# Four modulation blocks asked for at once, and x behind them, at the start of a flow-matching layer kernel

## The reference, cut to what matters

```python
def layer(x, cond, k_ctx, v_ctx, w_ada, b_ada, w_in, ...):
    mods = (jax.nn.silu(cond) @ w_ada + b_ada)[:, None, :]
    sh1, sc1, ga1, sh2, sc2, ga2 = jnp.split(mods, 6, axis=-1)
    u = x * (1 + sc1) + sh1
    xc, bg, cg, q, k, v, g_conv, g_na = jnp.split(u @ w_in, IN_SPLITS, axis=-1)
    ...  # gated convolution, attention, merge by gates, w_o, layer norm
    x = layer_norm(ALPHA * x + ga1 * (merged @ w_o), ln1_g, ln1_b)
    u2 = x * (1 + sc2) + sh2
    x = layer_norm(ALPHA * x + ga2 * peer(u2, w_query, sub_keys, expert_u, expert_v), ln2_g, ln2_b)
```

## Time and profile before

| | us |
|---|---|
| median of 3 runs | 1949.89 |
| lowest and highest run | 1946.81, 1951.14 |
| span of the profiled execution | 1975.1 |
| TensorE busy in it | 1811.1 (92%) |
| VectorE busy in it | 1291.4 (65%) |
| GpSimd busy in it | 908.3 (46%) |
| ScalarE busy in it | 283.3 (14%) |
| moved by DMA in it | 670.23 MB, 339 GB/s on average |

### The profile page before, as it was taken

One profiled execution on the slowest core, in us unless ns is written; L12 is line 12 of the kernel. 1 busy time (PEld: TensorE's weight loads), 2 busy tenths in 40 slices (PEclk: granted clock), 3 DMA queues, 4 the chain that ended last, 5 costly groups with the idle time before them and its releaser, 6 DMA issues.

```text
span 1975.1 us, 21712 instructions
## 1 busy us (share of the span) xinstructions
PE 1811.1 (92%) x8148; PEld 1170.2 (59%) x8148; DVE 1291.4 (65%) x2583; ACT 283.3 (14%) x660; POOL 908.3 (46%) x837
## 2 busy tenths in 40 slices
PE   4888899967999899999999999998799899995997
PEld 2676744446544349997888888886544334442443
DVE  2110487879688778999988966549956533349752
ACT  0120010037300001111110100016620000000000
POOL 1010226668555412235454566657856664545500
PEclk8998999989999999999999999999999999997999
DMA  8894949898999967469999999997999999999983
GB/s 355 355 365 189 356 178 407 290 369 274 337 398 336 346 241 286 140 217 376 346 374 379 370 409 409 409 372 267 336 354 409 410 407 409 409 409 410 409 326 135
DMA packets 166713, 670.23 MB, mean 339 GB/s; under 512 B 19370, under 2 KB 19498, under 8 KB 160972
## 3 DMA queue, kind: packets, MB, share of 16 engines
q0 software_dynamic: 112512, 410.79, 55.1%
q1 hardware_dynamic: 49344, 242.24, 31.3%
q10 hardware_dynamic: 4752, 15.81, 2.1%
HBM read 659.27 MB, written 7.39 MB: 338 GB/s over the span
## 4 chain that ended last, share of the span: by engine, by line
PE 65%; DMA 13%; DVE 8%; POOL 7%; issue 4%; another core or an unknown queue 2%; ACT 1%; ACTq 0%; SPq 0%; DVEq 0%; POOLq 0%
PE psum L853 22%; PE psum L921 16%; PE psum L1014 7%; DMA arena<-in_expert_u_dram,arena 7%; POOL arena L542 7%; PE psum L979 4%; PE psum L944 3%; PE psum L947 3%; DVE arena L1425 3%; PE psum L881 2%; DMA arena<-in_w_ada_dram 2%; PE psum L956 1%; PE psum L954 1%; PE psum L698 1%
## 5 line engine op out<-in xcount | busy, mean ns | idle before, releaser
L542 POOL DMA_INDIRECT arena<-in_expert_u_dram,arena x384 | 487.2, 1269 | 349.7 <-DVE arena L1425 219.5
L1425 DVE CUSTOM_DVE_ANT_0 arena<-arena 128x1024 f32<-128x1024 f32 x384 | 460.5, 1221 | 182.4 <-DMA arena<-in_expert_u_dram,arena 172.1
L542 POOL DMA_INDIRECT arena<-in_expert_v_dram,arena x384 | 382.3, 996 | 375.5 <-DVE psum L1659 208.6
L921 PE MATMUL psum<-arena 128*128 128x512 f32 x1024 | 451.4, 602 | 24.9 <-issue 16.9
L853 PE MATMUL psum<-arena 128*128 128x256 f32 x2048 | 445.9, 381 | 4.9 <-DMA arena<-in_expert_uT_dram 4.9
L1659 DVE SCALAR_TENSOR_TENSOR psum<-arena,psum 128x1024 f32<-128x1024 f32 x254 | 327.0, 1287 | 162.1 <-DMA arena<-in_expert_v_dram,arena 132.0
L853 PEld LDWEIGHTS psum<-arena 128*128 128x128 f32 x2048 | 390.7, 191 | 58.8 <-issue 5.2
L921 PEld LDWEIGHTS psum<-arena 128*128 128x128 f32 x1024 | 196.2, 193 | 281.1 <-issue 272.0
L1014 PE MATMUL psum<-arena 128*128 128x128 f32 x1280 | 149.8, 278 | 3.6 <-issue 3.1
L1014 PEld LDWEIGHTS psum<-arena 128*128 128x128 f32 x1280 | 147.3, 195 | 5.4 <-issue 4.7
L710 PE MATMUL psum<-arena 128*128 128x512 f32 x320 | 137.7, 592 | 0.0
(11 more groups left out here) (174 smaller groups left out, 1352.1 us busy)
## 6 DMA issues: line engine op xcount, KB each, us to landing
arena<-in_expert_uT_dram SPq DMA_DIRECT2D x128, 512.0 KB
arena<-in_expert_v_dram SPq DMA_DIRECT2D x128, 512.0 KB
arena<-in_w_in_dram SPq DMA_DIRECT2D x16, 2048.0 KB
arena<-in_w_ada_dram SPq DMA_DIRECT2D x12, 2048.0 KB
arena<-in_w_query_dram SPq DMA_DIRECT2D x8, 2048.0 KB, 22.9
arena<-in_w_in_dram SPq DMA_DIRECT2D x16, 512.0 KB, 8.7
arena<-in_w_o_dram SPq DMA_DIRECT2D x4, 2048.0 KB
arena<-in_expert_u_dram,arena POOLq DMA_INDIRECT x384
```

Source lines behind the costliest of these rows:

```text
L542: pool.indirect_dma_start(slot, None, table[0], bass.IndirectOffsetOnAxis(ap=number, axis=0)).then_inc(land, 16)
L921: mm = pe.matmul(bank(2 + 2 * d + hf), own, RINGS[value_load_of(n) % RING][:, hf * HALF:(hf + 1) * HALF], start=n == 0, stop=n == NKEYS - 1)
L1425: dve.tensor_tensor_reduce(UR[b], UR[b], U2B[e], 1.0, 0.0, ALU.mult, ALU.add, DOTS[e % 2][:, k:k + 1]).then_inc(u_free, 1)
```

## The change

The fourth modulation block gets the place at offset 31744, and is left out of the turns of the three slots. SyncE no longer waits for the small inputs. GpSimd waits for the small inputs as before, and then for the fourth modulation block, before it asks for x.

```diff
+SPARE = ("ada", 3)
...
         slot_of, before, last, counts, landed = {}, {}, {}, [0] * (WSLOTS + 1), {}
-        for n, key in enumerate(loads):
-            slot = n % WSLOTS
+        turns = [key for key in loads if key != SPARE]
+        for key in loads:
+            n = WSLOTS if key == SPARE else turns.index(key)
+            slot = WSLOTS if key == SPARE else (n + (n >= turns.index(("in", 1, PROJ[0])))) % WSLOTS
             if key[0:2] == ("query", 1):
                 slot = (2, 3, 0, 1)[key[2]]
...
         @block.sync
         def _(sp):
-            sp.wait_ge(cond_in, 48)
             for key in loads:
...
-                if slot_of[key] == 3:
+                if slot_of[key] == WSLOTS and key != SPARE:
                     sp.wait_ge(merge_done, 16)
...
             pool.dma_start(MODS, b_ada[0:1, :].partition_broadcast(2)).then_inc(bada_in, 16)
             pool.wait_ge(cond_in, 48)
+            pool.wait_ge(w_land[WSLOTS], 16)
             for k in range(KD):
                 pool.dma_start(UT[:, k, :], xT[k * P:(k + 1) * P, :]).then_inc(x_in, 16)
```

## The result

The changed kernel takes 1958.62 us in the median of 7 runs, the kernel before 1949.89 in 7 runs: a ratio of 1.0039, with a 95% interval of 1.0027 to 1.0051, so slower by 7.6 us (5.3 to 9.9); the two medians lie 8.7 us apart. Ratios compare fast executions alone, so one of e7 (3199 us, at a clock of 0.556) and one of the kernel before (1985 us) are not in them. I had forecast 1953.8 with a range of 1948.0 to 1958.5: the right side, half the size. By the ratio the changed kernel stands at 1957.5, inside the range; its median is 0.1 us above the range's end.

The account below looks back on a forecast made before the run. An unbroken chain of waits starts with full DMA engines, the first projection needing modulation and x. Extra bytes ahead of x, 8.8 us, less 4.9, plus about 0.1, delay L1358 by 3.9 us: median 1953.8, range 1948.0 to 1958.5.

Parts of the forecast that it names:

- Rival B: Loads before the first projection: x passes the backlog and lands at 35.1 us; 1945.3 us, faster; chance 0.10.
- rival C: DMA queues: equal bytes instead of equal packets, x lands at 41.4 us; +1.7 us, 1951.6; chance 0.10.
- A: The forecast itself, at the start: x lands last, queues shared packet by packet; range 1950.5 to 1957, chance 0.70.
- D: Start: small inputs held up so long that blocks lie unused and engines may idle; 1956.8 at 22 us; chance 0.03.
- E: Start: x's tail runs slower alone and the clock is the worse case; +5.5 + 1.6 us, 1957; chance 0.07.
- Part 1: SyncE's first request: without the wait it moves from 5.67 to 0.75 us, 4.9 us earlier for every byte.
- Part 2: Small inputs sharing the engines: complete at about 13 us, 19 at worst; no cost as long as x is later.
- Part 3: x behind block 3: 17.30 MB must move before it lands, at 43.7 us; L1358 begins at 43.8, +3.9 us.
- Part 4: in0, in1 and ada 4 landing before x: buys nothing; DMA stands still some 13 us instead of 5.
- Part 5: TensorE's clock in the first projection: between a gain of 1.2 us and a cost of 1.6, taken as zero.
- Part 7: Latent blocks: the first, asked for at 233.86 us, lands at 241.4, before TensorE needs it at 243.55; no effect.
- The rigid chain: Whole kernel: an unbroken chain of waits, so a shift of the first projection is a shift of the end.

Follow-up runs that it names:

- e7: The changed kernel with SyncE's wait for the small inputs put back and GpSimd's wait for block 3 removed; ratio to the kernel before 0.9999 [0.9973, 1.0026].
- e6: The changed kernel with SyncE asking for in1, and so ada 4, only when all of x has landed; ratio to the kernel before 0.9993 [0.9971, 1.0015].
- e1: The changed kernel with SyncE's wait for the small inputs put back; ratio to the kernel before 1.0046 [1.0028, 1.0065].
- e4: The changed kernel with the conditioning on a semaphore of its own, apart from selector and unit matrix; ratio to the kernel before 1.0039 [1.0019, 1.0058].

## Why the prediction was right in its direction and too small

- *The two things that start u, and x last.* Right. L1361 is released by x, 12.17 us after the modulation; e6 gives 10 us back by moving two blocks behind x, and e1 against e7 shows that x's place behind block 3 makes it land 9.5 us later with the small inputs on time. Rival B (x passes the backlog) and rival C (equal bytes) are ruled out by 49.08 and by the packets: from 40 to 43 us SyncE's queue had 58 (0.95 MB) and GpSimd's 62 (0.28 MB). What came true was A's mechanism together with D's gap, to which I had given 0.03, and E's slow tail, 0.07; 1957.5 lies above the 1957 that A alone was to reach.
- *Part 1, 4.9 us earlier for every byte.* Failed as a gain: e1 against after shows 0.45 us, e1 against e4 3.15 us even with the small inputs' chain untied.
- *Part 2, the small inputs at about 13 us.* This step failed. They came at 20.4, past the 19 us I had named as the end, which was the full count of one large packet for each small one. I had taken a third of their packets to be through before the weights' data flowed; in fact none was: even the conditioning, asked for at the same moment as block 0, took 9.5 us instead of 1.6. This is the condition of rival D, with A's mechanism beside it, and it costs the gap of 2.7 us.
- *Part 3, the sum of bytes at 0.42 MB per us.* The mechanism was right, its size short by 2.6 us: 2.0 are the tail, in which x was alone and the engines ran at 226 to 298 GB/s on average, and on which I had put "under 1 us"; 0.6 are bytes not counted. x was also asked for at 25.63 and not at 23.6. Together: 43.8 + 2.7 + 2.6 = 49.1; the 2.7 and the 2.6 are e4's, so that they add up follows from how they were taken.
- *Part 4, the early blocks buy nothing.* Right: DMA (last two columns below) stood still from x's landing to the request at 63.14.
- *Part 5, the clock.* Within its bounds. From 50.0 the projection took until 63.14, 13.1 us where it took 12.2, with the lower level, 0.50 of the clock, held past 58.2 us:
```profile
52.80:58.20 5.40, 5.40 (x22) 4.77 (x22) 2.07 (x6) 0.00 (x0) 0.00 (x0) 0.50 0.00 0
58.20:63.10 4.90, 4.90 (x39) 4.90 (x39) 0.00 (x0) 0.00 (x0) 0.00 (x0) 0.83 0.00 0
```
  Against the earlier trace rows, 42 matmuls in 4.70 us are 39 in 4.90 now. By the later modulation the difference is gone again (the table's fourth column).
- *Part 7, the latent blocks.* Right. The first is asked for at 241.79 and TensorE goes on without a wait:
```profile
249.64 2.01 PE L1005 MATMUL psum<-arena 128*128 128x128 f32 x16
251.48 10.89 PE L713 MATMUL psum<-arena 128*128 128x512 f32 x25
```
- *What I took as the kernel before's start of u, 39.96, was a lucky execution.* A second profile has 41.94. By 243 us the two profiles agree within 0.2 us, so of the 9.1 us at the start of u some 7.5 count, and it is this that the median shows. My 3.9 was short by the errors of parts 2 and 3, 5.3 us at the start of u, and some 1.6 us of the lucky start were lost again further on.
- *The rigid chain.* Right: the changed kernel is 7.3 to 8.1 us late at 243 us, and 6.8 to 7.7 late at 501 us.

What stays open: the tail of x alone was seen but not tried by itself. The queue is not slow as long as all engines are busy (394 GB/s); that some of the 16 engines end their share of x before others fits the falling share, but no view here tells the engines apart.

## What to carry to other kernels

When the DMA engines are full, ask early for nothing that can wait, if the next stage waits for something else: sum the bytes that stand in front of it, in all queues, and put what is needed later behind it. An earlier request of large blocks delays the small inputs beside them; give the one that the first work needs a semaphore of its own. Judge a change at the start by the time at which the stage begins, in several profiles, and not by the span of one.

## What the runs showed that I had not expected

Small transfers beside large ones were slow by the count of their packets: 27 packets for each engine, of 4 to 512 bytes each, had all landed 18.7 us after the last request beside packets of 16 KB, and after 4.0 us without the weights. And TensorE's clock was not the same at the same place: in two executions of the kernel before and one of e7, in which the fourth block landed within 0.3 us of the same time, after the same 3.6 us of idle, its 16 matmuls took 1.92, 2.75 and 3.64 us (granted clock 1.00, 0.67 and 0.50). With the sums behind them this moved the start of u by up to 2.8 us with no change in their work, and by the first latent projection the three stood at 243.55, 243.35 and 243.94 us again.
